# A two-layer hybrid transformer on one core: a loads' order, a fourth buffer, the end of the mLSTM, the first MLP quarter of layer 1 and the sink's sum

## The reference, cut to what matters

```
h = rms_norm(x, g1) * (1 + sc1) + sh1              # sc, sh, ga: modulation, c @ w_mod
z = h @ w_in                                       # 17 parts
o_a = global attention (4 heads, RMS-normed, rotated q and k)
o_b = window attention (|i - j| <= 128) with a sink logit in the softmax
o_c = gated linear attention (GLA), two directions
o_d = mLSTM, two directions: y = sigmoid(o) * rms_norm(h, g_mlstm)
x = x + ga1 * ([o_a, o_b, o_c, o_d] @ w_out)
x = x + ga2 * (relu((rms_norm(x) * (1 + sc2) + sh2) @ w_mlp1) ** 2 @ w_mlp2)
```

## Time and profile before

| | |
|---|---|
| median of 3 runs | 1770.73 us (1767.09 to 1772.96) |
| the profiled execution | 1768.33 us, its span 1766.5 us |
| PE busy | 1673.9 us (95%), x11814 |
| DVE busy | 1165.0 us (66%) |
| ACT busy | 861.1 us (49%) |
| POOL busy | 267.4 us (15%) |
| granted TensorE clock, mean | 0.984 |

### The profile page before, as it was taken

How to read it: one execution, slowest core, us unless ns; L and a number is a source line. 1 busy time by engine, 2 the same in 40 slices (tenths; PEclk the granted TensorE clock), 3 DMA queues, 4 the chain that set the end, 5 groups by cost and what they waited for, 6 DMA issues and landing times. The chain is left out here.

```text
span 1766.5 us, 29062 instructions
## 1 busy us (share of the span) xinstructions
PE 1673.9 (95%) x11814; PEld 1483.8 (84%) x11814; DVE 1165.0 (66%) x1580; ACT 861.1 (49%) x1372; POOL 267.4 (15%) x212
## 2 busy tenths in 40 slices
PE   6999999989899999999999989999898989999998
PEld 4779898767778999999999968879677787989897
DVE  5466546666538897886986966754767494747472
ACT  5333325646317664555546573332655284527161
POOL 0233641401110000000000024352311200000000
PEclk8999999999999999999999999999999999999999
DMA  9541113200146548358177024222300346546351
GB/s 386 146 176 49 49 49 108 96 1 2 68 171 230 223 149 319 141 203 312 68 286 267 29 99 137 73 108 82 134 1 1 119 188 242 202 157 251 107 191 48
DMA packets 45457, 250.28 MB, mean 142 GB/s; under 512 B 5998, under 2 KB 7452, under 8 KB 26652
## 3 DMA queue, kind: packets, MB, share of 16 engines
q1 hardware_dynamic: 43420, 245.49, 37.4%
q10 hardware_dynamic: 1920, 3.15, 0.5%
HBM read 218.73 MB, written 26.74 MB: 139 GB/s over the span
## 5 line engine op out<-in xcount | busy, mean ns | idle before, releaser
L888 POOL TENSOR_TENSOR w_lo<-raw,w_hi 128x512 fp32r<-128x512 f32 x124 | 178.9, 1474 | 933.8 <-ACT w_hi L1028 912.1
L3622 PE MATMUL ps<-op_hi,w_hi 128*128 128x384 f32 x880 | 298.3, 339 | 5.8 <-ACT x_add L1616 2.8
L3622 PE MATMUL ps<-op_hi,w_lo 128*128 128x384 f32 x880 | 295.7, 336 | 0.0
L3622 PE MATMUL ps<-op_lo,w_hi 128*128 128x384 f32 x880 | 295.7, 336 | 0.0
L3622 PEld LDWEIGHTS ps<-op_hi,w_hi 128*128 128x128 f32 x880 | 165.4, 188 | 13.0 <-issue 7.4
L3622 PEld LDWEIGHTS ps<-op_lo,w_hi 128*128 128x128 f32 x880 | 165.5, 188 | 0.0
L3622 PEld LDWEIGHTS ps<-op_hi,w_lo 128*128 128x128 f32 x880 | 165.4, 188 | 0.0
L1576 ACT ACTIVATE w_hi<-raw 128x1024 fp32r<-128x1024 f32 x96 | 102.0, 1065 | 125.3 <-PE ps L3622 64.8
L1490 ACT ACTIVATE w_hi<-raw 128x1024 fp32r<-128x1024 f32 x80 | 82.6, 1053 | 135.4 <-PE ps L3585 118.2
L2697 DVE TENSOR_TENSOR w_lo<-raw,w_hi 128x1024 fp32r<-128x1024 f32 x96 | 116.4, 1220 | 22.2 <-ACT w_hi L1576 22.0
L3293 PE MATMUL ps<-w_hi,h_hi 128*128 128x256 f32 x448 | 130.1, 290 | 0.0
(11 more groups left out here) (414 smaller groups left out, 3973.0 us busy)
## 6 DMA issues: line engine op xcount, KB each, us to landing
raw<-w_big SPq DMA_DIRECT2D x96, 1024.0 KB, 6.1
raw_m<-w_modl SPq DMA_DIRECT2D x21, 1024.0 KB, 6.3
op_hi<-op_cache SPq DMA_DIRECT2D x21, 768.0 KB, 4.8
op_lo<-op_cache SPq DMA_DIRECT2D x21, 768.0 KB, 6.5
raw<-w_modl SPq DMA_DIRECT2D x14, 1024.0 KB, 4.9
op_hi<-op_cache SPq DMA_DIRECT2D x21, 512.0 KB, 4.2
op_lo<-op_cache SPq DMA_DIRECT2D x21, 512.0 KB, 6.1
first_mod<-w_modl SPq DMA_DIRECT2D x8, 1024.0 KB, 20.9
```

Source lines behind the costliest of these rows:

```text
L888: ins = nc.gpsimd.tensor_tensor(w_lo[r][:, ks, :], src[:, ks, :], w_hi[r][:, ks, :].bitcast(F32), ALU.subtract)
L3622: ins = mm(bank(base + g, 0, h), wide(w)[:, k, g * P:(g + 1) * P], ops[hl][:, k, 0:h], start=(p in FRESH and k == 0 and q == 0), stop=(k = ...
```

## The change

What it does, in five parts.

- **Order of transfers.** In the in-projection's loop on SP the weight is loaded behind the modulation of m = 0 and ahead of that of m = 1. In layer 0's out-projection the third modulation is loaded ahead of two MLP blocks, and the one that goes into `raw_m` is issued when the one before has landed, not when it has been summed.
- **Four buffers** for the attention's squares: ACT squares first and then issues the swap, which waits for `turned`, not for `normed`. `normed(l, 5)` moves ahead of `tokens` of the last group. The buffers' places change.
- **The sink's sum.** L1955 goes; ACT takes `exp(sink + nb)` itself, two instructions of 128x1 per unit of m = 1 in place of one of 128x4 per two units.
- **End of the mLSTM.** `low_ab(1)` goes ahead of `outputs(END_S)`; the multiplication with the gate goes to POOL (`gate_d`), ahead of its last weights' low parts; features 5 and 4 are split ahead of the root and the last multiplication; PE turns `y_d` ahead of k = 5, not of k = 6.
- **Layer 1's first MLP quarter.** `s1_1(0)` goes to POOL, `s2_1(0)` to its place at the head of `norm_mlp`; the first `t_sum1` and `high_a1(2)` come earlier; `hid_low1(1)` goes behind the eviction of product 5; `part_group` waits by pairs of k.

The diff, with little context and less indentation:

```
@@ -77,6 +77,7 @@
 GATE_U = 4
+RABS = 4
@@ -180,7 +181,6 @@
 gqk_swap = keep("gqk_swap", [4])
-se = keep("se", [2, 4])
@@ -275,10 +275,10 @@
 ms_d = place("ms_d", mod_acc_at + 640, [TILES * 4])
-rab = [place(f"rab{i}", RX + i * TB, [T]) for i in range(3)]
-rt = [place(f"rt{i}", RX + 3 * TB + i * 2048, [SEQ]) for i in range(3)]
-st = [place(f"st{i}", RX + 5 * TB + i * 2048, [SEQ]) for i in range(3)]
-prob_first = place("prob_first", RX, [2, T])
+rt = [place(f"rt{i}", RX + i * 2048, [SEQ]) for i in range(3)]
+st = [place(f"st{i}", RX + 2 * TB + i * 2048, [SEQ]) for i in range(3)]
+rab = [place(f"rab{i}", RX + (4 + i) * TB, [T]) for i in range(RABS)]
+prob_first = place("prob_first", RX + 6 * TB, [2, T])
@@ -419,6 +419,10 @@
 return sum(len(att_pairs(i)) for i in range(l + 1))
+def sinks_to(l, u):
+
+return sum(m for i in range(l) for m, _, _ in att_pairs(i)) + sum(m for m, _, _ in att_pairs(l)[:u + 1])
@@ -665,8 +669,8 @@
                     load_mod(mslot(in_mod(l, s + 1, m)))
-            if w0 + s != PROJ:
-                load_w(wslot(d0 + s + 2), w0 + s + 2)
+                if m == 0 and w0 + s != PROJ:
+                    load_w(wslot(d0 + s + 2), w0 + s + 2)
@@ -749,17 +753,20 @@
             continue
+        load_mod(mslot(out_mod(l, 2)))
...
         load_block("22", 0, 0)
-        load_mod(mslot(out_mod(l, 2)))
...
         sp.wait_ge(sem("d_ready"), 1)
-        load_mod(mslot(out_mod(l, OUT_MODS[0] - 1)), raw_m)
+        sp.wait_ge(sem("mod_landed"), 16 * (mods.n - 1))
+        sp.dma_start(raw_m[:], mslot(out_mod(l, OUT_MODS[0] - 1))).then_inc(sem("mod_landed"), 16)
+        sp.wait_ge(sem("mod_summed"), mods.at(0))
+        mods.add()
@@ -991,6 +998,14 @@
         add_outputs(END_S - 1)
+    def gate_d(l):
+
+        nj = n_q(l) // P
+        gp.wait_ge(sem("gate_ready"), 2 * (l + 1))
+        gp.wait_ge(sem("sqd_ready"), l + 1)
+        yd = y_d[:, 0:nj, :]
+        nc.gpsimd.tensor_tensor(yd, yd, ro[:, 0:nj, 256:512], ALU.mult).then_inc(sem("yd_gated"), 1)
@@ -1000,7 +1015,13 @@
         mlstm(l)
+        gate_d(l)
         lows(l * PROJ + IN_SLOTS + 2, (l + 1) * PROJ)
+    gp.wait_ge(tile_landed("22"), TILE1 + 16)
+    gp.wait_ge(sem("mw_sum"), SUM1 + 2)
+    for c_ in range(2):
+        at = chunk(raw21, c_)
+        nc.gpsimd.tensor_tensor(at, at, chunk(raw22, c_), ALU.add).then_inc(sem("mw_sum"), 1)
@@ -1110,10 +1131,12 @@
                 high_w(2, 0)
+                if l == 1:
+                    high_second()
...
                 keep_first(1)
-            elif k == 4:
+            elif k == 4 and l == 0:
@@ -1284,20 +1307,22 @@
         act.wait_ge(sem("ft_ready"), FEATS * l + 8 + i)
+        if i >= RABS:
+            act.wait_ge(sem("qk_ready"), 6 * l + i + 1 - RABS)
+        nc.scalar.activation(rab[i % RABS][:, 0:n], ft[i][:, 0:n], ACT.Square).then_inc(sem("sqab_ready"), 1)
         if i >= 3:
-            act.wait_ge(sem("qk_ready"), 6 * l + i - 2)
+            act.wait_ge(sem("turned"), 6 * l + i - 2)
...
             nc.scalar.dma_start(st[i % 3][x::2, :], ft[i][1 - x::2, 0:SEQ]).then_inc(swap_landed(l, i)[0], 16)
-        nc.scalar.activation(rab[i % 3][:, 0:n], ft[i][:, 0:n], ACT.Square).then_inc(sem("sqab_ready"), 1)
...
         act.wait_ge(sem("msab_ready"), 6 * l + i + 1)
-        nc.scalar.activation(rab[i % 3][:, 0:n], bank(4, 0, n), ACT.Ln, bias=eps[:, 0:1],
+        nc.scalar.activation(rab[i % RABS][:, 0:n], bank(4, 0, n), ACT.Ln, bias=eps[:, 0:1],
...
         act.wait_ge(sem("lnab_done"), 6 * l + i + 1)
-        nc.scalar.activation(rab[i % 3][:, 0:n], rab[i % 3][:, 0:n], ACT.Exp,
+        nc.scalar.activation(rab[i % RABS][:, 0:n], rab[i % RABS][:, 0:n], ACT.Exp,
@@ -1387,9 +1412,12 @@
                 probs(l, u, 1, a0, b0)
-            if m == 1 and p == 1:
-                nc.scalar.activation(es[:, u // 2 % 2, :], se[:, u // 2 % 2, :],
-                                     ACT.Exp).then_inc(sem("es_ready"), 1)
+            if m == 1:
+                for hb in range(2):
+                    h = p + 2 * hb
+                    ins = nc.scalar.activation(es[:, u // 2 % 2, 2 * p + hb:2 * p + hb + 1], rowc[:, h:h + 1], ACT.Exp,
+                                               bias=nb[:, u % 2, hb:hb + 1], scale=1.0)
+                ins.then_inc(sem("es_ready"), 1)
@@ -1464,9 +1492,10 @@
         nc.scalar.activation(sq_d[:, 0:nj, :], y_d[:, 0:nj, :], ACT.Square).then_inc(sem("sqd_ready"), 1)
-        act.wait_ge(sem("msd_ready"), l + 1)
-        rsqrt_mean(ms_d[:, 0:nj * 4]).then_inc(sem("rstdd_ready"), 1)
         for i, k in enumerate(TURNS):
+            if i == 2:
+                act.wait_ge(sem("msd_ready"), l + 1)
+                rsqrt_mean(ms_d[:, 0:nj * 4]).then_inc(sem("rstdd_ready"), 1)
@@ -1944,16 +1973,16 @@
             dve.wait_ge(sem("exp_done"), e0 + 2 * u - 2)
+            if att_pairs(l)[u - 2][0] == 1:
+                dve.wait_ge(sem("es_ready"), sinks_to(l, u - 2))
...
                                  negate=True))
-            step(v.tensor_tensor(nb[:, u % 2, hb:hb + 1], mx[:, u % 2, hb:hb + 1], nsink[:, h:h + 1],
-                                 ALU.min))
-            v.tensor_tensor(se[:, u // 2 % 2, 2 * p + hb:2 * p + hb + 1], nb[:, u % 2, hb:hb + 1], rowc[:, h:h + 1],
-                            ALU.add).then_inc(ready, 1)
+            v.tensor_tensor(nb[:, u % 2, hb:hb + 1], mx[:, u % 2, hb:hb + 1], nsink[:, h:h + 1],
+                            ALU.min).then_inc(ready, 1)
@@ -1973,6 +2002,7 @@
                     maxima(l, 0, 1, T_("sca").n, T_("scb").n, T_("exp").n)
+                    normed(l, 5)
@@ -2079,7 +2109,7 @@
             turned(l, i)
-        if 1 <= i < 7:
+        if 1 <= i < 6:
@@ -2259,9 +2289,9 @@
         dve.wait_ge(sem("rab_ready"), 6 * l + i + 1)
-        ins = v.tensor_tensor(ft[i][:, lat], rt[i % 3][:], rab[i % 3][:, lat], ALU.mult)
+        ins = v.tensor_tensor(ft[i][:, lat], rt[i % 3][:], rab[i % RABS][:, lat], ALU.mult)
         if n_q(l) == T or i not in Q_FEATS:
-            ins = v.scalar_tensor_tensor(ft[i][:, ctx_], ft[i][:, ctx_], g, rab[i % 3][:, ctx_],
+            ins = v.scalar_tensor_tensor(ft[i][:, ctx_], ft[i][:, ctx_], g, rab[i % RABS][:, ctx_],
@@ -2287,7 +2317,7 @@
             if m == 1:
-                dve.wait_ge(sem("es_ready"), T_("es").add())
+                dve.wait_ge(sem("es_ready"), sinks_to(l, 2 * jj + 1))
@@ -2403,11 +2433,12 @@
                 sums(s)
+        dve.wait_ge(sem("inter_done"), inter_n(l, END_S, 1))
+        low_ab(1)
...
         dve.wait_ge(sem("yd_ready"), out_n(l, END_S, 1))
-        dve.wait_ge(sem("inter_done"), inter_n(l, END_S, 1))
-        for k in range(1, 4):
-            low_ab(k)
+        low_ab(2)
+        low_ab(3)
@@ -2419,15 +2450,15 @@
                             yT_hi[:, k, 0:n].bitcast(F32), ALU.subtract).then_inc(sem("y_lo"), 1)
-        dve.wait_ge(sem("gate_ready"), 2 * (l + 1))
...
                         AX_X, ALU.add).then_inc(sem("msd_ready"), 1)
-        step(v.tensor_tensor(yd, yd, ro[:, 0:nj, 256:512], ALU.mult))
-        dve.wait_ge(sem("rstdd_ready"), l + 1)
-        yd = yd.rearrange("p j (h c) -> p (j h) c", c=64)
-        v.tensor_tensor(yd, yd, bc(ms_d[:, 0:nj * 4], 64), ALU.mult).then_inc(sem("d_ready"), 1)
         for i, k in enumerate(TURNS):
+            if i == 2:
+                dve.wait_ge(sem("rstdd_ready"), l + 1)
+                dve.wait_ge(sem("yd_gated"), l + 1)
+                yd = yd.rearrange("p j (h c) -> p (j h) c", c=64)
+                v.tensor_tensor(yd, yd, bc(ms_d[:, 0:nj * 4], 64), ALU.mult).then_inc(sem("d_ready"), 1)
@@ -2444,7 +2475,7 @@
     land.n = 16
-    def norm_mlp(l, n_t, first_sums, low_first, low_second, late_sums):
+    def norm_mlp(l, n_t, first_sums, low_first, low_second):
@@ -2476,9 +2507,7 @@
             if k == 3:
-                late_sums(0)
                 low_second()
-        late_sums(1)
@@ -2508,7 +2537,7 @@
                         ALU.subtract).then_inc(sem("op_lo"), 1)
-    def t_sum1(n):
+    def t_sum1(n, scaled=0):
@@ -2518,7 +2547,7 @@
         if n == 1:
-            dve.wait_ge(sem("h_mlp"), T_("hm").n - 4)
+            dve.wait_ge(sem("h_mlp"), T_("hm").n + scaled - 4)
@@ -2542,7 +2571,7 @@
             dve.wait_ge(sem("big_done"), big1(q, 0, 0))
-        dve.wait_ge(sem("mw_sum"), SUM1 + 8 * q + 2)
+        dve.wait_ge(sem("mw_sum"), SUM1 + 8 * q + (2 if q else 4))
@@ -2622,11 +2651,14 @@
                 s4_1(q, 1)
-            if P_ == (3 if q else 5):
+            if P_ == 3 and q:
...
                 evict1(P_, 0)
+            if P_ == 5 and q == 0:
+                hid_low1(1, 0)
+                hid_low1(1, 1)
@@ -2907,14 +2939,14 @@
                 low_w1(0, 1, 1)
+                t_sum1(1, 2 * KD)
...
             def first_sums1():
-                s1_1(0, 0)
-                s1_1(0, 1)
-
-            norm_mlp(l, n_t, first_sums1, lambda: low_w1(0, 1, 0), low_second1, lambda c_: s2_1(0, c_))
-            t_sum1(1)
+                s2_1(0, 0)
```

(13 more changed lines are left out.)

## The result

The changed kernel takes 1746.26 us in the median of 4 runs (1744.71 to 1747.80), the kernel before 1769.29 beside it (1767.09 to 1772.96): ratio 0.9868, 95% interval 0.985 to 0.9885. The forecast was 1746. (The sum as written gives 1745.4 + 1.2 = 1746.6, not 1746.)

A forecast was written before the change was run, and what follows sets the result against it. PE, busy for 1673.9 of 1766.5 us, was taken as the bound, with only its gaps at stake. Terms of 22.95 off 1768.33 gave 1745.4, and with half of 2.4 added, 1746; 8 in 10 range 1737 to 1757.

The forecast's parts named there:

- transfers: Layer 0's in-projection and out-projection: PE's waits for modulations go; gains 2.8 (0 to 2.8) and 2.85 us (1.5 to 4.05).
- four buffers, normed: Layer 1's last square and the head of attention in both layers: PE's waits shrink, gain 3.4 us (0.5 to 6.4).
- sink: Attention's wide units: second exponent 0.33 us earlier without two L1955, at most 5.3 us over 16 waits; 4.5 taken.
- end of the mLSTM: Out-projection's first slots: of 8.2 us of waits for low parts, 1.1 comes back in layer 1; gain 7.1 (3 to 8.2).
- first quarter: Layer 1's first MLP quarter: 1.1 + 0.5 + 1.6 of waits go, 0.9 charged; gain 2.3 us (-1 to 4).
- rival 2: Gaps cost more than they show: closing them also ends most low-clock stretches, 6 us more, 1739; chance 0.11.
- ahead of the eviction it is done in layer 1 before PE ends the group, so 1.6 of 1.8 goes: Head of attention: `normed(l, 5)`, moved ahead of the last group's eviction, saves PE 1.6 us in layer 1, 0.6 in layer 0.
- rival 1: Gains in chains of small instructions return as the next wait, above all in attention and first quarter: 1757; chance 0.21.
- sign of being wrong: In attention: waits of `values` for L1378 or L1381, ACT's evictions behind the new exponents, would show the forecast wrong.
- the forecast's one meeting: First quarter: the addition of squares at 1409.7 overlaps POOL's work, costing about 1.1 us, within over 1 us of slack.
- 3: Rival: slower, the altered rhythm lowers the clock through the attention loops, 1.42 us per unit, 1802 at worst; chance 0.03.
- 4: Rival: SP's or POOL's new waits are met no earlier, only the order changes; gain under 5 us, 1766; chance 0.05.

The follow-up runs named there:

- wo_sink: The changed kernel with the sink's sum again on VectorE (L1955, `se` and one exponent of 128x4 back): 1746.30 us, 0.9859 of the kernel before.
- a_pad: The changed kernel with an unused buffer of 32 bytes where `se` stood, so activations lie at the old addresses: 1740.49 us, 0.9834 of the kernel before.
- b_again: The kernel before once more, nothing changed, for a second trace: 1770.14 us in its one run.
- wo_buf: The changed kernel with three buffers for the squares and `normed(l, 5)` behind `tokens`, as before: 1749.13 us, 0.9876 of the kernel before.
- wo_end: The changed kernel with the mLSTM's end as before (old order, gate on DVE): 1755.34 us, 0.9921 of the kernel before.

## Why the prediction was right, step by step

| term | forecast, us | runs | what the stages show |
|---|---|---|---|
| transfers | 2.8 + 2.85 | 8.3 | 5.9 in one trace, 4.5 in two; 2.4 + 0.8 |
| four buffers, normed | 3.4 | 2.9 | 3.1 + 0.7 - 1.3 |
| sink | 4.5 | 5.8 | 3.6 + 3.3 (wo_sink against a_pad), each uncertain by 1.6 |
| end of the mLSTM | 7.1 | 9.1 | 4.9 + 3.8 (before against a_pad) |
| first quarter | 2.3 | 2.3 | 3.0 |
| address | none | -5.8 | a_pad against after |
| sum | 22.95 | 22.6 | measured 23.0 |

Each difference of two medians is uncertain by some 3 us, and each part was undone with the others in place; that the sum closes to 0.4 us is better than it can be known. By the ratios the column reads 8.3, 1.4, 4.4, 9.4, 0.7 and -6.0, 18.2 in all, against 23.4 measured.

**Transfers: the place right, the size too small.** The order worked as said: no wait near 113 us, none for a transfer in the out-projection, and ACT's norm late by 1.6 in place of the 1.8, of which the stage gained 0.5 (0.6 forecast). The in-projection's term was priced at its wait, 2.8, as its upper end too. The gap took 4.5 to 5.9, since the clock fell behind it. That was rival 2's mechanism, "the gaps cost more than they show". It was written with 6 us for the whole and so isn't the forecast's. Both traces of before have it: behind the wait of 2.77 the window 116 to 126 had 0.83, and behind the 2.76 of b_again it had 0.92.

**Buffers: the waits right, the head of attention wrong.** The failed step is "ahead of the eviction it is done in layer 1 before PE ends the group, so 1.6 of 1.8 goes". The two waits of 0.70 and 2.75 in layer 1 went but for 0.13 (I had left 0.9 and charged 0.7), and the one ahead of scores(1) rose to 3.12. After, around it, and the maximum of before:

```profile
1231.22 0.59 PE L3286 MATMUL ps<-ft,ft 64*128 64x512 f32 x1
...
1235.09 1.82 DVE L1979 TENSOR_REDUCE nb<-ps 128x1 f32<-128x768 f32 x2
1236.83 0.68 DVE L2292 TENSOR_TENSOR ft<-rt,rab 128x512 f32<-128x512 f32 x1
1236.97 0.89 ACT L1348 ACTIVATE prob_first<-ps,nb 128x768 f32<-128x768 f32 x1
...
1237.96 0.48 PE L3279 MATMUL ps<-ft,ft 64*128 64x256 f32 x1 [3.12 <-ACT prob_first L1348]
```

```profile
1254.25 1.82 DVE L1948 TENSOR_REDUCE nb<-ps 128x1 f32<-128x768 f32 x2 [1.70 <-PE ps L3254]
```

The scores are there at 1231.8, DVE takes their maximum at 1235.09. In between it has the rotation of the sixth feature. Before, that rotation ended at 1251.95, PE began these scores only at 1252.08, and DVE stood idle for 1.70 until they were there. PE is early now and DVE is not: rival 1, in this one place, for 1.3 us. That is read from the traces of after and wo_buf; a list of DVE with less in it there wasn't tried. What stands behind the wait costs more in most executions: in all nine other traces with such a wait (3.08 to 3.30) the granted clock of layer 1's attention was 0.96 to 0.98, where after, before and b_again had 1.00, and with the sink's part the loop took 72.8 to 74.1 us against 72.23. That the length of the wait brings this isn't shown: wo_buf, with 1.78 there, has 0.98 and 73.05 too.

**Sink: right by its steps.** After, in a wide unit (us, engine, instruction, [idle <- releaser]):

```profile
385.41 0.82 DVE L1982 TENSOR_REDUCE mx<-ps 128x1 f32<-128x640 f32 x1 [1.68 <-PE ps L3286]
...
387.43 0.79 ACT L1348 ACTIVATE prob<-ps,nb 128x640 f32<-128x640 f32 x1
388.12 0.19 ACT L1348 ACTIVATION_READ_ACCUMULATOR prob<-ps,nb 128x1 f32 x1
388.21 0.47 ACT L1418 ACTIVATE es<-rowc,nb 128x1 f32<-128x1 f32 x2
```

The second exponent starts 2.02 us behind the first maximum (2.38 before, 2.05 forecast), and the pair of new exponents takes 0.47, where the forecast reckoned with two of 0.19, some 0.1 apart. PE's waits behind it fell by 4.4 us. For the rest of the 5.8 the clock may stand: 1.00 over layer 0's loop in after and a_pad, 0.98 in wo_sink, 0.95 and 0.97 in the two traces of before. But five of the ten traces with the part have 0.98 there too, so this rest isn't shown to be the part's. One sign of being wrong did come: waits of `values` for ACT's eviction, two of 0.8 us together, which are too small to change the sum. A price that came with it stood in no term: taking `se` away moved every activation by 32 bytes.

**End of the mLSTM: right, sized too small by 2.** In layer 1 0.67 us came back at one place (forecast 1.1 at two), in layer 0 nothing. GpSimd's gate beside DVE:

```profile
1340.90 2.41 POOL L1007 TENSOR_TENSOR y_d<-y_d,ro 128x1024 f32<-128x1024 f32 x1 [4.14 <-ACT sq_d L1494]
1340.91 1.21 DVE L2454 TENSOR_REDUCE ms_d<-sq_d 128x16 f32<-128x1024 f32 x1
1342.04 1.28 DVE L2450 TENSOR_TENSOR yT_lo<-ps,yT_hi 128x512 fp32r<-128x512 f32 x2
...
1343.41 1.23 DVE L2461 TENSOR_TENSOR y_d<-y_d,ms_d 128x1024 f32<-128x1024 f32 x1
```

It takes 2.41 and in layer 0 3.57 (2.36 and 3.4 forecast) and ends at 1343.31, 0.1 us ahead of DVE's last multiplication: the cover was as thin as forecast, and enough. Undoing the part costs 10.4 us by stages, where it closes waits of 4.3 + 4.0 - 0.7: again a fall of the clock, in wo_end's layer 0. Against the two traces of before, which have no such fall there, it is 8.7.

**First quarter: right in the sum, not in the parts.** The waits of 1.63 and 1.94 fell to 0.58 and 1.53 (1.1 and 0.5 forecast), the second matrix's from 2.52 to 0.90 (1.6), and a new one of 1.13 came at 1417.82 for a low part. The first product starts 0.13 us later behind the out-projection's end (0.9 charged). By its letter that meets a condition under which the prediction said that it fails, "if the first quarter's products start later than now relative to the end of the out-projection"; the condition was ill chosen, since the sum itself charged 0.9 for it.

**DVE beside POOL.** L2450 inside GpSimd's gate takes 1.28 us for two, outside of it 1.29; it reads PSUM and one buffer of SBUF. The squares' addition, with two inputs in SBUF, ran beside the two sums of the first quarter:

```profile
1380.68 5.18 POOL L1024 TENSOR_TENSOR raw<-raw,raw 128x1024 f32<-128x1024 f32 x2 [9.53 <-DVE raw L2592]
1381.23 0.63 ACT L1079 ACTIVATE tmp<-xT 128x512 f32<-128x512 f32 x1 [4.80 <-DVE xT L2470]
1381.90 1.74 DVE L1899 TENSOR_TENSOR tmp<-tmp,tmp 128x512 f32<-128x512 f32 x1 [0.70 <-ACT tmp L1079]
```

1.74 us instead of 0.69 alone (at 1409.68 before), and POOL's pair 5.18 instead of 4.72: the forecast's one meeting, with its price of 1.1, inside the slack. A second one wasn't foreseen: L2485, with two inputs in SBUF, took 0.91 us at 1384.98, inside the pair, where 0.16 was taken before. The rule of the Trainium skill ("GPSIMD Engine Reference", Specifications), contention where VectorE's instruction has two SBUF inputs, agrees with these cases. That some 3 us would go by it did not come true, since the low parts that met the gate have one such input.

**Rivals.** 1 came true in one place, for 1.3 us. 2 came true in the transfers' term and may hide in the sink's. 3 and 4 did not: both attention loops are shorter, at a granted clock of 1.00 in the trace of after and 0.96 and more in the others. Without the address the time would have been 1740.5, at the edge of the forecast's own range and near rival 2's.

## What to carry to other kernels

Removing a small buffer moves all behind it: compare the distance of equal matmuls before and after, and keep the old addresses with an unused buffer while you judge an edit. Judge a part by its own stage in the trace, by leave-one-out at one address, and not by the total alone. Judge a stage's difference by how far the same code differs between traces, and look where inside the stage it arises. Price a gap of 2 us and more on PE with a range that reaches to twice its length, and ask, where a wait goes, which engine was catching up during it.

## What the runs showed of the hardware

- The pace of fp32 matmuls depends on the byte address at which the operands begin, to 32 bytes: 512 columns 0.2290 or 0.2333 us, 384 columns 0.1734, 0.1738, 0.1760 or 0.1767, over the run 6 to 15 us of 1750. The best of four places was the one with remainder 64 to 128, not the one at a multiple of 256. The weights and the other buffers ahead of the shift stayed where they were, so whether the address itself counts or the distance to them is open, and so is the rule by which the four places differ.
- At one place one line ran at 0.1133 or at 0.1178 us from one execution to the next, at a granted clock of 1.00 throughout, 4.5 us in all. Its cause is open; the execution, the chip and the program weren't told apart.
- Gaps of 2.75, 2.76, 2.77 and 2.08 us were followed by windows of 10 us with a granted clock of 0.77, 0.92, 0.83 and 0.83, and the first three cost 5.9, 4.5 and 4.5 us in all; gaps of 1.97 and 2.25 in the trace of before and of 3.12 after were not. But the gap at the same place as the 3.12 was followed by a low stretch in all nine other traces that have one over 3 us there. What decides it is open.
- The fastest version is the changed kernel with 32 unused bytes, 1740.49 us, 0.9834 of the kernel before.
